# Dilated prompt attention: TensorE takes an item's value products ahead of a later item's scores

## What is computed

```python
    sc = jnp.einsum('bgnqhd,bgnkhd->bgnhqk', qs, kb).astype(jnp.float32) / math.sqrt(HEAD_DIM)
    ...
    m = jnp.max(sc, axis=-1, keepdims=True)
    pw = jnp.exp(sc - m)
    l = jnp.sum(pw, axis=-1, keepdims=True)
    o = jnp.einsum('bgnhqk,bgnkhd->bgnqhd', (pw / l).astype(v.dtype), vb)
    lse = (m + jnp.log(l))[..., 0]
```

## Time and profile before

| | us |
|---|---|
| median of 3 runs | 3746.33 (3744.97 to 3747.36) |
| the profiled execution: its time | 3739.83 |
| its span | 3738.3 |
| TensorE busy in the span | 3111.2 (83%) |
| VectorE busy | 1753.4 (47%) |
| ScalarE busy | 1445.0 (39%) |

### The profile page before, as it was taken

One profiled execution on the slowest core, in us unless ns is written; L12 is line 12 of the kernel. 1 busy time (PEld: TensorE's weight loads), 2 busy tenths in 40 slices (PEclk: granted clock), 3 DMA queues, 4 the chain that ended last, 5 costly groups with the idle time before them and its releaser, 6 DMA issues. The chain is left out here.

```text
span 3738.3 us, 54015 instructions
## 1 busy us (share of the span) xinstructions
PE 3111.2 (83%) x17296; PEld 2117.0 (57%) x17296; DVE 1753.4 (47%) x3170; ACT 1445.0 (39%) x3010; POOL 721.4 (19%) x1297
## 2 busy tenths in 40 slices
PE   5999599996888888897999578788877666489998
PEld 4888478884444444446788455444554222168887
DVE  2000222224888888885565334333432222456663
ACT  3222322224666666665555223232332111333332
POOL 0000022222434343430000023333332000000000
PEclk9999799997999999998999789898987777789999
DMA  4444634443010100005322399999997232332321
GB/s 148 158 160 158 200 110 157 167 172 112 1 35 1 35 1 12 1 1 134 92 63 61 87 353 385 385 384 370 386 381 266 87 124 90 127 114 98 111 102 36
DMA packets 315636, 547.78 MB, mean 147 GB/s; under 512 B 65402, under 2 KB 159066, under 8 KB 312316
## 3 DMA queue, kind: packets, MB, share of 16 engines
q1 hardware_dynamic: 272892, 343.54, 27.5%
q0 software_dynamic: 42496, 201.23, 14.6%
HBM read 484.95 MB, written 126.68 MB: 164 GB/s over the span
## 5 line engine op out<-in xcount | busy, mean ns | idle before, releaser
L392 PE MATMUL proj_ps_G<-proj_w_hi,proj_xT_hi 128*128 128x512 f32 (+1 forms) x1088 | 427.9, 393 | 49.1 <-DVE proj_xT_lo L288 49.1
L1201 POOL DMA_DIRECT2D sbs_v_ring<-in_cache_v_sb x512 | 275.6, 538 | 897.7 <-issue 895.9
L396 PE MATMUL proj_ps_G<-proj_w_hi,proj_xT_lo 128*128 128x512 f32 (+1 forms) x1088 | 425.0, 391 | 0.0
L394 PE MATMUL proj_ps_G<-proj_w_lo,proj_xT_hi 128*128 128x512 f32 (+1 forms) x1088 | 424.9, 391 | 0.0
L1448 PE MATMUL sbs_ps_T<-sbs_ident,sbs_k_ring 128*128 128x128 f32 x2048 | 296.7, 307 | 97.3 <-DMA sbs_k_ring<-in_cache_k_sb 81.6
L1287 DVE COPY sbs_kT<-sbs_ps_T 128x512 f32<-128x512 f32 x256 | 176.2, 688 | 415.2 <-PE sbs_ps_T L1448 414.9
L1448 PEld LDWEIGHTS sbs_ps_T<-sbs_ident,sbs_k_ring 128*128 128x128 f32 x2048 | 265.7, 160 | 138.6 <-DMA sbs_k_ring<-in_cache_k_sb 89.3
L355 ACT ACTIVATE proj_out<-proj_ps_G,proj_stat 128x512 f32<-128x512 f32 (+1 forms) x136 | 93.7, 689 | 598.8 <-PE proj_ps_G L396 598.8
L519 POOL CAST sbp_sp_hi<-sbp_sp 128x512 fp32r<-128x512 f32 (+3 forms) x320 | 236.9, 740 | 313.1 <-DVE sbp_sp L550 300.6
L288 DVE TENSOR_TENSOR proj_xT_lo<-proj_ps_T,proj_xT_hi 128x512 fp32r<-128x512 f32 (+1 forms) x68 | 42.2, 662 | 541.8 <-ACT proj_xT_hi L345 541.8
L612 ACT ACTIVATE sbp_el<-sbp_el 128x512 f32<-128x512 f32 (+3 forms) x320 | 180.1, 567 | 232.9 <-DVE sbp_el L545 231.5
(11 more groups left out here) (258 smaller groups left out, 5966.9 us busy)
## 6 DMA issues: line engine op xcount, KB each, us to landing
sbs_v_ring<-in_cache_v_sb POOLq DMA_DIRECT2D x512, 256.0 KB, 5.9
sbs_k_ring<-in_cache_k_sb SPq DMA_DIRECT2D x512, 256.0 KB, 9.8
out_k_win_s<-in_cache_k_win POOLq DMA_DIRECT2D x16, 2044.0 KB
out_v_win_s<-in_cache_v_win POOLq DMA_DIRECT2D x16, 2044.0 KB
proj_out<-in_w_in SPq DMA_DIRECT2D x32, 512.0 KB, 5.6
proj_x_in<-in_x_prompt SPq DMA_DIRECT2D x32, 512.0 KB, 3.6
dls_k_in<-in_cache_k_win SPq DMA_DIRECT2D x16, 1024.0 KB, 7.4
dls_v_in<-in_cache_v_win SPq DMA_DIRECT2D x16, 1024.0 KB
```

The lines of the kernel that those rows point to most:

```text
L392: nc.tensor.matmul(ps_G[0:n, g, :], xT_hi[:, slot, k, 0:n], w_hi[:, k, cols], start=(k == 0), stop=False)
L394: nc.tensor.matmul(ps_G[0:n, g, :], xT_hi[:, slot, k, 0:n], w_lo[:, k, cols], start=False, stop=False)
L396: mm = nc.tensor.matmul(ps_G[0:n, g, :], xT_lo[:, slot, k, 0:n], w_hi[:, k, cols], start=False, stop=(k == KC - 1))
L1201: eng.dma_start(ring[:, q % RING, i, :], cache[bass.ds(page, 1), :, :].rearrange("a s c -> (a s) c")) \
```

## The change

In TensorE's loop, `weigh(g - 1)` now stands between `turn_weights(g)` and `score(g + 2)`. It stood behind `score(g + 2)`. No instruction is added or removed, and no wait; the other engines' queues are as they were.

```diff
             for g in range(-2, G + 2):
                 if 0 <= g < G:
                     turn_weights(g)
+                if 0 <= g - 1 < G:
+                    weigh(g - 1)
                 if g + 2 < G:
                     score(g + 2)
-                if 0 <= g - 1 < G:
-                    weigh(g - 1)
                 if 0 <= g - 2 < G:
```

## The result

The changed kernel takes 3806.4 us (median of 4 runs, 3803.0 to 3811.8) against 3745.7 for the kernel before: a ratio of 1.0163 (95% interval 1.0145 to 1.0180), slower. The forecast was 3804, slower, with a range of 3786 to 3836. All times here are medians of fast executions; a single execution of one later kernel (value products ahead of the transposes), which took 4548.7 us at a mean granted clock of 0.65, is left out.

A forecast was written before the change was run, and what follows sets the result against it. TensorE was taken to bound the stage. Waits of 38.4 and 8.9, plus 4.6 and 1.9 at the pairs' ends, sum to 53.8 us; with 4 for the clock, 3746.3 becomes 3804 us, range 3786 to 3836.

The forecast's parts named there:

- What bounds the stage: TensorE, busy 375.7 of 396 us in the stage, sets the pace; order wins nothing unless a wait goes away.
- The new wait: Value products that open a group wait for `take_out`: 30 times 1.28 us, and 8 times 1.11 in the last pair.
- TensorE's blocks themselves cost the same: In every iteration, one passage from score products to a block of another shape before and after; no added time.
- The clock: In dilation 16, five more iterations with value products at the lower level, 0.88 us each: 4 us added.
- the 4.6 and 1.9 of the forecast: Pairs' ends, first three pairs: 4.6 us for scores now behind item 18's store wait, 1.9 for the store starting later.
- The stores: At the pairs' ends, 10.77 us from `put_out(15)` to the reductions, taken as unchanged.
- the narrow range: Forecast case, 3788 to 3815 us, from 1.1 to 1.45 us per wait and 0 to 10 for the clock; chance 0.76.
- Rival 1: The clock falls at every new wait: 38 value products at 1.97 instead of 1.09 add 33 us, 3833; chance 0.15.
- Rival 2: No wait appears at the moved value products, so the time would be 3746 us; chance 0.05.
- Rival 3: Earlier `put_out(15)` shrinks the three long store waits at pairs' ends, 16.5 us gone: 3730; chance 0.04.

## Why the prediction was right, and where it was lucky

- **What bounds the stage** was right. No experiment that left TensorE's blocks and the store's wait as they were came below 3741.
- **The new wait** was right in place, count and size: 1.29 and 1.11 us more in the iterations concerned outside dilation 16, where 1.28 and 1.11 were forecast, in the items named. Item 17 of the first three pairs waits too (1.26 to 1.30 us), ahead of the longer wait for the store, where the forecast had it covered. Taking one VectorE step out of the chain took 0.60 to 0.63 out of each wait; taking all out removed it.
- **"TensorE's blocks themselves cost the same"** was the step that failed. It counted only the passages away from score products. The 0.20 us per iteration, some 15.6 in sum, come from value products between transposes and mask products; the rows to see it were at hand, since the earlier trace rows give 0.80 from transposes to masks and the earlier trace rows a passage from transposes to value products that keeps only 0.04 of overlap.
- **The clock** was mis-sized with the wrong sign. I added 4 us, for five more value products of dilation 16 at 1.97; there is none of them above 1.38 in the changed kernel, and together they take 4.2 us less than before. I also counted some five iterations as cold already, where the trace of the kernel before has seven value products above their length at the full clock. The terms as measured are 38.7 + 8.9 for the waits, 15.6 for the blocks, the 4.6 and 1.9 of the forecast, and 2.9 less at the stores (next point); they make 66.8, the stage has 60.4. The trace shows where the 6.4 between them lie: the 16 iterations of dilation 16 last 6.8 us longer than before, where their eight waits and 16 x 0.20 would make 13.2; all others last 53.6 us longer, and their terms make 53.6. The rows above show one way it goes: transposes at the lower level ahead of a shortened wait. But in the profiled executions of five kernels without any new wait and without the 0.20 (`take_out` first in the kernel before, masks ahead with `take_out` first, and the three with the store's wait late) these 16 iterations last between 3.6 us less and 1.7 us more than in the kernel before, so part of the 6.4 can be chance.
- **The stores** were taken as 10.77 us from `put_out(15)` to the reductions in all three pairs. This holds in the first pair before only (1801.26 to 1812.03). The second and third have 7.97 (1901.11 to 1909.08) and 8.27, and in the changed kernel the three have 7.89 (1816.93 to 1824.82), 8.24 and 7.99: 27.0 us in sum before, 24.1 after. In the long one SyncE took 4.87 us to issue the four stores of the outputs, in the changed kernel 2.29. This goes with the order: in the seven kernels whose value products all stand ahead of the scores it is 2.29 to 2.36 in the first pair, in the five others 2.74 to 5.81. Why was not tried. The first pair's end, SyncE's timeline, before and then changed:

```profile
1801.98 4.87 SPq L860 DMA_DIRECT2D scratch_o_dil<-dil_o_out  x4
```

```profile
1817.64 2.29 SPq L860 DMA_DIRECT2D scratch_o_dil<-dil_o_out  x4
```

- So 3804 against 3806.4 is closer than its parts: 15.6 too little in one place, some 10 and 3 too much in two others. That is luck. And the lower end of the narrow range, 3788, does not follow from its own terms: 1.1 us per wait (0.93 in the last pair) and nothing for the clock give 3793.
- **Rival 1** (the clock falls at every wait) fell: 1.00 in the windows over the waits, value products at 0.88 and 1.09. The loop that the Trainium skill tells of ("TensorE: Matmul & The Clock Gate", section "HAM oscillation — how this bites in real kernels") waits about 3 to 5 us for a DMA in every turn, so it need not have held for waits of 1.28, as the prediction had it; here it does not arise with waits of 1.2 to 1.3 us. **Rival 2** fell with the 42 new waits. **Rival 3** fell: in the second pair `put_out(15)` began 8.08 us after item 17's transposes (1925.02 to 1933.10, a new wait within) and not 5.94, and the three waits still sum to 15.0 us (4.86, 5.21, 4.97).

## What to carry to other kernels

Ahead of moving an instruction forward in an in-order queue, follow what it waits for through the other engine's queue: here a VectorE chain of two or three steps, harmless behind the scores, came to stand on the path some 40 times; work that doesn't need the wait belongs ahead of the waiting instruction (moving the two mask products there took 35 of the 61 us back). A wait should stand at the first instruction that touches the buffer in question: moving one such wait by a few items gained 20 us, more than any order of the blocks.

## What the runs showed of the hardware

- Eight transposes of 128x128 in f32 hand on to mask products after 0.79 to 0.80 us (0.85 if they themselves stand behind value products), to value products (weights of 64 columns) only after 0.96 to 0.97; four transposes hand on to transposes after 0.50, to value products after 0.59. Behind mask products the value products cost nothing extra: the iteration has its 4.66 us again.
- Idle gaps of 1.2 to 1.3 us every 9 to 11 us left the granted clock at 1.00 over 62 us, while in dilation 16 it fell to 0.57 with no idle time (1792 to 1796 us of the kernel before). What in dilation 16 brings it down was not tried.
